# Attention scores of several heads computed side by side on TensorE, each head into a PSUM bank of its own

## The reference

```
# local attention: 6 query heads of 64 over 2 key/value heads, ALiBi, window 128, a sink per head
scores = einsum(q, k) * 64**-0.5 + bias          # head h uses key/value head h // 3
p = exp(scores - m); probs = p / (sum(p) + exp(sink - m))
out_a = probs @ v
# differential attention: 4 heads, each with two query/key maps of 32 and one value of 64
a = softmax(einsum(q, k) * 32**-0.5 - slope * dist)    # for both maps
out_c = rms_norm((a[0] - lam * a[1]) @ v) * (1 - lambda_init)
# the third mixer is a bidirectional state space model (Mamba-2): conv, decays, chunks of 128
x = x + concat(out_a, out_b, out_c) @ w_out
x = x + experts(rms_norm(x))
```

## Time and profile before

| | us |
|---|---|
| median of 3 runs | 1340.1 |
| the three runs | 1339.53, 1340.10, 1346.42 |
| profiled execution, its own time | 1351.05 |
| its span, first to last instruction | 1349.3 |
| TensorE busy (matmuls) | 1016.5 (75% of the span) |
| VectorE busy | 382.1 (28%) |
| ScalarE busy | 191.6 (14%) |
| mean granted clock of TensorE | 0.885 of full speed |
| DMA: bytes moved, mean rate | 437.50 MB, 324 GB/s |

### The profile page before, as it was taken

One profiled execution on the slowest core, in us unless ns is written; L12 is line 12 of the kernel. 1 busy time (PEld: TensorE's weight loads), 2 busy tenths in 40 slices (PEclk: granted clock), 3 DMA queues, 4 the chain that ended last, 5 costly groups with the idle time before them and its releaser, 6 DMA issues.

```text
span 1349.3 us, 26710 instructions
## 1 busy us (share of the span) xinstructions
PE 1016.5 (75%) x11124; PEld 639.6 (47%) x11124; DVE 382.1 (28%) x1160; ACT 191.6 (14%) x549; POOL 9.1 (1%) x28
## 2 busy tenths in 40 slices
PE   5999977766667887767679999766775767766864
PEld 5877753333334443334358777534432433333432
DVE  4456451211212222111144465512111111111112
ACT  2144210000000111000021443100000000000001
POOL 2000000000000000000000000000000000000000
PEclk9899989878888999977979999779877888888887
DMA  9822129999999989799993220289999999999992
GB/s 324 343 93 84 45 88 367 425 424 424 426 426 424 404 335 426 310 403 414 411 377 125 74 115 33 94 347 425 424 425 425 425 424 424 424 426 426 424 419 115
DMA packets 46015, 437.50 MB, mean 324 GB/s; under 512 B 8064, under 2 KB 10112, under 8 KB 21248
## 3 DMA queue, kind: packets, MB, share of 16 engines
q1 hardware_dynamic: 45824, 434.72, 78.1%
HBM read 433.65 MB, written 1.05 MB: 322 GB/s over the span
## 4 chain that ended last, share of the span: by engine, by line
PE 58%; DMA 22%; issue 13%; DVE 5%; ACT 1%; DVEq 1%; ACTq 0%
DMA ring<-in_w_up 22%; PE ps L465 20%; PE ps L537 7%; PE ps L476 7%; PE ps L485 4%; PE ps L446 4%; PE ps L654 4%; PE ps L549 2%; PE ps L609 2%; PE ps L583 1%; PE ps L594 1%; PE ps L553 1%; PE ps L453 1%; PE ps L616 1%; PE ps L633 1%
## 5 line engine op out<-in xcount | busy, mean ns | idle before, releaser
L465 PE MATMUL ps<-ring,xg 128*32 128x256 f32 x4096 | 337.7, 487 | 240.6 <-issue 173.3
L465 PEld LDWEIGHTS ps<-ring,xg 128*32 128x32 f32 x4096 | 173.2, 138 | 386.5 <-issue 348.7
L943 DVE SCALAR_TENSOR_TENSOR gu<-th,ps 128x128 f32<-128x128 f32 x72 | 20.7, 287 | 704.1 <-ACT th L750 704.1
L476 PE MATMUL ps<-ring,actT 128*32 128x256 f32 x2304 | 139.2, 382 | 15.2 <-issue 12.9
L750 ACT ACTIVATE th<-ps 128x128 f32<-128x128 f32 x72 | 20.0, 277 | 609.5 <-PE ps L465 609.5
L476 PEld LDWEIGHTS ps<-ring,actT 128*32 128x32 f32 x2304 | 69.0, 109 | 76.3 <-issue 20.5
L537 PE MATMUL ps<-hT,ring 128*128 128x256 f32 x416 | 97.6, 395 | 1.3 <-DVE hT L993 1.3
L537 PEld LDWEIGHTS ps<-hT,ring 128*128 128x128 f32 x416 | 81.4, 199 | 13.5 <-ACT aneg L788 2.1
L446 PE MATMUL ps<-xh,Pb 128*32 128x256 f32 x1024 | 81.1, 400 | 2.4 <-issue 2.4
L485 PE MATMUL ps<-ysb,PwT 32*128 32x256 f32 x1024 | 75.5, 404 | 2.5 <-issue 1.5
L485 PEld LDWEIGHTS ps<-ysb,PwT 32*128 32x128 f32 x1024 | 47.3, 186 | 32.5 <-issue 29.0
(11 more groups left out here) (249 smaller groups left out, 831.5 us busy)
## 6 DMA issues: line engine op xcount, KB each, us to landing
ring<-in_w_gate SPq DMA_DIRECT2D x64, 2048.0 KB, 23.7
ring<-in_w_up SPq DMA_DIRECT2D x64, 2048.0 KB, 25.1
ring<-in_w_down SPq DMA_DIRECT2D x64, 2048.0 KB, 19.3
ring<-in_w_in SPq DMA_DIRECT2D x8, 2048.0 KB, 19.2
ring<-in_w_out SPq DMA_DIRECT2D x4, 2048.0 KB, 19.7
ring<-in_w_in SPq DMA_DIRECT2D x2, 1584.0 KB, 14.6
x<-in_x SPq DMA_DIRECT2D x1, 1024.0 KB, 5.1
out<-fin SPq DMA_DIRECT2D x2, 512.0 KB, 2.7
```

The costliest lines, as they stand in the source:

```text
L465: last = mm(b_gate[j * SLOTS:(j + 1) * SLOTS, 0:2 * GQ], tokens[:, k, :], ring[:, low:high + 1:high - low, o:o + GQ], start=(k == 0), stop ...
L476: last = mm(b_y[j * SLOTS:(j + 1) * SLOTS, 0:DQ], actT[:, c * SLOTS:(c + 1) * SLOTS], ring[:, slot, o:o + DQ], start=(c == 0), stop=(c == ...
```

## The change

The scores leave the steps `sc.u` on TensorE. Five new steps compute them in groups: `aS.0` to `aS.2` two local heads each, one from each key/value head, so on array rows 0 to 63 and 64 to 127; `cS.0` and `cS.1` four units of two differential heads each, on the four groups of 32 rows. Within a group the matmuls alternate between the units, and each unit writes its own bank. VectorE and ScalarE keep their steps `sc.u`, in the old order; VectorE's now waits for the whole group.

Local unit `u` is now head `HEAD[u]` (0, 3, 1, 4, 2, 5), so that two units in a row come from both key/value heads. The two heads of an `oa` step then no longer fill one block of `mixT`, and ScalarE copies the two halves apart. Banks no longer go round: a step takes the bank whose last reader comes first in `ORDER`, and a group may hold several. `pT.6` moves ahead of the second differential group.

```diff
 ORDER = """
...
-    cv nm.5 oa.0 ybn pT.4 pT.5 sc.7 oa.1 yT.0 sc.8 nm.6 yT.1 oa.2 sc.9 sc.10 nm.7 sc.11 pT.6 outA.0 sc.12 pT.7
+    cv nm.5 oa.0 ybn pT.4 pT.5 sc.7 oa.1 yT.0 sc.8 nm.6 yT.1 oa.2 pT.6 cS.1 sc.9 sc.10 nm.7 sc.11 outA.0 sc.12 pT.7
...
+HEAD = [i % A_KV * REP + i // A_KV for i in range(A_H)]
+def tenants(step):
+    if step[0] == "aS":
+        return [("sc", A_KV * step[1] + i) for i in range(A_KV)]
+    if step[0] == "cS":
+        return [("sc", A_H + 4 * step[1] + i) for i in range(4)]
+    return [step]
+def read_at(tenant):
+    at = AT[tenant]
+    if tenant[0] == "pT" and tenant[1] >= 2:
+        h = tenant[1]
+        at = max(at, AT["oa", min(h // 2 - 1, 2)] if h < A_H + 2 else AT["od", h - A_H - 2])
+    return at
...
-        BANK[_s] = _n % 8 if _i < FIRST_OUT else 4 + _n % 4
+            _b = min(range(0 if _i < FIRST_OUT else 4, 8), key=lambda k: (read_at(_held_by[k]) if k in _held_by else -1, k))
+        BANK[_t] = _b
+        if _b in _held_by and _s[0] != "outB":
+            HELD.setdefault(_s, []).append(_held_by[_b])
+        _held_by[_b] = _t
...
+                    elif kind == "aS":
+                        if s[1] == 0:
+                            pe.wait_ge(done["act"], nth(li, "act", ("ak",)))
+                        for t in range(TT):
+                            for g in range(A_KV):
+                                r = slice(g * A_D, (g + 1) * A_D)
+                                last = mm(ps[BANK["sc", A_KV * s[1] + g]][:, t * SEQ:(t + 1) * SEQ],
+                                          aqT[r, s[1], t * P:(t + 1) * P], akT[r, :], start=True, stop=True)
+                    elif kind == "cS":
+                        pe.wait_ge(done["act"], nth(li, "act", ("ck", s[1])))
+                        for t in range(TT):
+                            for i in range(4):
+                                r = slice(i * C_QK, (i + 1) * C_QK)
+                                last = mm(ps[BANK["sc", A_H + 4 * s[1] + i]][:, t * SEQ:(t + 1) * SEQ],
+                                          cqT[r, s[1], t * P:(t + 1) * P], ckT[r, s[1], :], start=True, stop=True)
...
-                        last = A(mixT[:, s[1], :], bank[:, 0:SEQ], ACT.Copy)
+                        for h in HEAD[A_KV * s[1]:A_KV * s[1] + A_KV]:
+                            half = slice(h % 2 * A_D, (h % 2 + 1) * A_D)
+                            last = A(mixT[half, h // 2, :], bank[half, 0:SEQ], ACT.Copy)
...
+                        dve.wait_ge(done["pe"], nth(li, "pe", ("aS", u // A_KV) if u < A_H else ("cS", (u - A_H) // 4)))
```

More of the change, by code:

```diff
@@ L100 @@
 STEPS = [(name, *map(int, index)) for name, *index in (step.split(".") for step in ORDER.split())]
-ON_PE = {"xT", "xbc", "dt", "cq", "aq", "ak", "cum", "xs", "cb", "row", "sc", "y", "vz", "pT", "ck", "cv", "oa", "od",
+ON_PE = {"xT", "xbc", "dt", "cq", "aq", "ak", "cum", "xs", "cb", "row", "aS", "cS", "y", "vz", "pT", "ck", "cv", "oa", "od",
          "yT", "cT", "outA", "outB", "fT", "lg", "seed", "rank", "ov"}
@@ L155, in reader @@
     return "dve" if step[0] in ("dt", "cum", "sc", "y", "lg", "rank", "ov") else "act"
+PE_STEPS = list(COUNT["pe"])
+FIRST_OUT = PE_STEPS.index(("outA", 0))
+AT = {step: i for i, step in enumerate(STEPS)}
+HEAD = [i % A_KV * REP + i // A_KV for i in range(A_H)]
[11 more added lines that the diff above has]
+    return at
+BANK, HELD = {}, {}
+_held_by = {}
+for _i, _s in enumerate(PE_STEPS):
+    if _s[0] == "seed":
+        continue
+    for _t in tenants(_s):
+        if _s[0] in ("outA", "outB"):
+            _b = _s[1]
+        elif _s[0] == "ov":
+            _b = 7
+        else:
+            _b = min(range(0 if _i < FIRST_OUT else 4, 8), key=lambda k: (read_at(_held_by[k]) if k in _held_by else -1, k))
[3 more added lines that the diff above has]
+        _held_by[_b] = _t
 def build_encoder(nc, x_in, cols, rows, w_in, w_out, w_router, w_gate, w_up, w_down, final_w, out):
@@ L502, in _ @@
                     bank = ps[BANK[s]] if s in BANK else None
-                    if s in HELD:
-                        held = HELD[s]
+                    for held in HELD.get(s, ()):
                         pe.wait_ge(done[reader(held)], nth(li, reader(held), held))
@@ L595, in _ @@
                                           start=(n == 0), stop=(n == 2))
[L596 to L607, removed]
-                        for t in range(TT):
-                            last = mm(bank[:, t * SEQ:(t + 1) * SEQ], ql[:, t * P:(t + 1) * P], kr, start=True, stop=True)
+                    elif kind == "aS":
+                        if s[1] == 0:
+                            pe.wait_ge(done["act"], nth(li, "act", ("ak",)))
+                        for t in range(TT):
+                            for g in range(A_KV):
[9 more added lines that the diff above has]
+                                          cqT[r, s[1], t * P:(t + 1) * P], ckT[r, s[1], :], start=True, stop=True)
                     elif kind == "pT":
@@ L621, in _ @@
                         pe.wait_ge(done["act"], nth(li, "act", ("pT", 2 * c + 1)))
-                        for half in range(2):
-                            h = 2 * c + half
+                        for g in range(A_KV):
+                            half = HEAD[A_KV * c + g] % 2
                             for kc in range(TT):
-                                g = h // REP
                                 last = mm(bank[half * A_D:(half + 1) * A_D, 0:SEQ], vz[:, kc, g * A_D:(g + 1) * A_D],
-                                          ptb[h % 2][:, kc, :], start=(kc == 0), stop=(kc == TT - 1))
+                                          ptb[g][:, kc, :], start=(kc == 0), stop=(kc == TT - 1))
                     elif kind == "od":
@@ L844, in _ @@
                         if u < A_H:
-                            last = A(nmx[:, 2, u, :], nmx[:, 1, u, :], ACT.Exp, bias=rowp[:, R_SK + u:R_SK + u + 1])
+                            last = A(nmx[:, 2, u, :], nmx[:, 1, u, :], ACT.Exp, bias=rowp[:, R_SK + HEAD[u]:R_SK + HEAD[u] + 1])
                     elif kind == "pT":
@@ L1122, in _ @@
                             dve.drain()
-                            last = v.tensor_scalar(nmx[:, 1, u, :], nmx[:, 0, u, :], -A_SCALE, nsink[:, u:u + 1],
+                            last = v.tensor_scalar(nmx[:, 1, u, :], nmx[:, 0, u, :], -A_SCALE, nsink[:, HEAD[u]:HEAD[u] + 1],
                                                    ALU.mult, ALU.min)
```

8 lines of the change are left out of this document (4 added, 4 removed).

## The result

The changed kernel took 1359.6 us (median; 1356.5 to 1366.4) against 1343.15 for the kernel before: a ratio of 1.013, with a 95% interval of 1.0075 to 1.0185. It is slower, 5.6 us above the forecast and inside its range. Measured again the ratio was 1.0123 (1.0093 to 1.0154).

What follows compares the result with a forecast made beforehand. Mixers bound by TensorE, expert stages of fixed length by transfers; 0.3 (ScalarE) + 4.0 (bank waits) + 2.7 (clock) = 7.0 us per layer, 14 in all, 1365 us profiled, 1354 at the median. Range 1343 to 1363.

Steps and rivals of the forecast that it cites:

- The groups: Score matmuls on TensorE: four units in one step cost about what one costs, 1.1 us.
- Rival C: Score groups on TensorE: row groups run one after the other, 1360 us; chance 0.03.
- rival A: TensorE: the seven saved slots per layer count in full, 15 us off, 1325 us; chance 0.06.
- `cv`: TensorE up to `cv`: it starts 2.4 us earlier, after waits for the decay rows and for unit 5's bank.
- ScalarE up to `outA.0`: ScalarE's stretch from `oa.0` to `outA.0`: -2.4 + 1.1 (`oa.1`) + 0.8 (half copies) + 0.75 (copy of `pT.6`), +0.3 us.
- rival B: ScalarE behind `oa.0`: copy of `pT.4` starts at once, `cv`'s cut reaches `outA.0`; not slower, 1343 us; chance 0.17.
- rival D: Clock at its upper bound, 5 us per layer, with `oa.1` and `cS.1` at half clock; 1361 us; chance 0.20.
- The waits in `outA`: TensorE waits for banks of units 12 and 13, 4.0 us ahead of `outA.1`, 2.1 ahead of `outA.2`; price +4.0 per layer.
- The clock: Half clock behind new TensorE waits: 1.7 us behind the wait of 4.0, 1.0 for the others, 2.7 per layer.
- Sum: Both layers: 0.3 + 4.0 + 2.7 = 7.0 us each, 14 us slower in all, 1354 us.
- The expert stage: Behind the mixers: fixed length set by transfers, so it passes on the mixers' shift and gives nothing back.

Runs made afterwards that it cites:

- e0: The changed kernel as it is, measured again; 1.0123 of the kernel before.
- e1: The changed kernel with units 10 to 13 of `cS.1` in banks 1, 2, 3, 5 instead of 3, 5, 1, 2; 0.9981 of the kernel before.
- e3: The changed kernel with eight unread matmuls in the wait ahead of `outA.1` and four ahead of `outA.2`; 1.0052 of the kernel before.
- e6: e5 with the matmuls of a group unit by unit, no longer turn by turn; one run, 1341.0 us.
- e5: e2 with `cS.1` moved ahead of `pT.6`; 0.9973 of the kernel before.
- e2: e1 with other banks also for `pT.5`, `pT.6`, `oa.1`, `yT.0` and `yT.1`; 0.9969 of the kernel before.
- e7: e5 with unread matmuls in TensorE's gaps, one ahead of `oa.2` and three ahead of `cS.1`; 0.9942 of the kernel before, again 0.9939.
- e4: The changed kernel with each `oa` copied once and whole instead of in two halves, result not that of the reference; one run, 1363.7 us.
- e8: The kernel before with two unread matmuls ahead of `pT.6`; 0.9979 of the kernel before.

## Why the prediction was right

I take its steps in their order. The mechanism held at each; the clock's term was too small, and so was the smaller one ahead of `outA.0`.

**The groups.** Forecast 1.1 us, measured 1.15 in the trace's duration, where a single unit has 1.13 (1.06 to the start of the next step); a group of two has 1.13 and 1.06 as well. The Trainium skill, "TensorEngine Tiling (Array Packing)", section Theoretical Speedup, gives up to 4x for a contraction of 32 rows; four units of 1.13 in 1.15 us are 3.9x, so the trace agrees. Rival C falls with it, and rival A does too: the speed was there and the time wasn't.

**`cv`.** Forecast 2.4 us earlier; measured 2.25 in the first layer (47.87 instead of 50.12 behind `cb.0`) and 1.9 in the second. The waits that I put there are there: 0.70 of `y.2` for the decay rows, and 0.29 and 0.66 of `cv` for unit 5.

**ScalarE up to `outA.0`.** Forecast +0.3, measured +0.49 and +1.32, and +0.57 to +1.54 in e0, e1 and e3, which have the same steps up to there. The delay by `oa.1` was 1.26 (forecast 1.1), and this refutes rival B, whose test was the start of that copy. A half copy costs 0.39 more and not 0.27, so the three cost 1.17 and not 0.8. The copy of `pT.6` ahead of `outA.0` took 0.60 and ended 0.05 before it. With these sizes the sum for the first layer is -2.25 + 1.26 + 1.17 + 0.75 = +0.9; where the other 0.4 went I haven't traced. In the second layer `oa.1` took 1.57 us and `cS.1` 1.74, partly at half clock, which I had given to rival D.

**The waits in `outA`.** Forecast 4.0 and 2.1, measured 3.77 and 1.93, in both layers and in both traces of the changed kernel. At full clock (e3) `outA.2` starts 19.20 us behind `outA.0`; forecast 19.5. The price of the stretch is 42.71 - 39.14 = 3.57 us per layer against the 4.0 forecast. By e1 the waits alone are worth 42.71 - 36.65 = 6.1, of which two saved slots and what goes with them give back 2.5. The Trainium skill, same page, section Restrictions and Gotchas, warns of the pressure on PSUM. The trace agrees in part: the group does hold four banks at once, but e1 holds the same four and loses nothing. The loss lies in which unit got which.

**The clock, the term that was mis-sized.** I took 2.7 us per layer, 5.4 in all. Behind `outA.0`'s start the changed kernel loses, against e3, 45.98 - 42.71 = 3.27 in the first layer and 5.86 in the second. Before had 1.69 of its own in the first, so the change adds 7.4. What was missing is `outB`: it too ran partly at half clock, 8.86 instead of 7.17 us in both layers, 3.4 in all, which I had not counted. Without it the change adds 4.1. A second error went the other way and hid part of the first: I doubled a layer that had no fall before, though the earlier trace rows showed one in the other, so I charged 1.7 us that before was paying already. The fall also reached the router's two steps of the first layer, which took 5.0 us longer (5.89 and 6.54 us instead of 3.73 and 3.70); the wait of 3.98 ahead of the ranking was gone in return, and the first gather came 1.0 us later behind `fT`, within the 568 us.

**Sum.** To `outA.0` 1.8 (forecast 0.6), waits 7.1 (8.0), clock 7.4 (5.4): 16.4 us against 14. The rest of the 5.6 us between forecast and median is the base: the runs of before that the forecast started from had a median of 1340.1, and later medians of the same kernel were 1343.15 to 1346.65. The ratio is the better measure of the forecast: 1354/1340.1 is 1.0104, and 1.013 and 1.0123 were measured. That the profiled execution (1361.93) came near the 1365 of the forecast is luck: from trace to trace the span grew by 10.9 us only, since 5.5 of the mixers' 16.4 were made up in steps that the change doesn't touch.

**The expert stage.** It took up nothing that the traces can show between the layers (568.06 and 567.93 us, in a scatter of some us). The last one, from its first gather to the end of the last matmul, was 466.4 us long and 468.4 before. I haven't traced these 2 us; one trace of each kernel can't tell them from chance.

## What to carry to other kernels

Steps that run side by side hold several banks at once. Give these by when each reader will be done, in the order of the reader's queue: here the same step with two pairs of banks exchanged was worth 1.4% of the kernel. A slot saved on a busy engine counts only until another engine's chain is late; look for the first step whose operand comes from elsewhere, and don't multiply slots by their length. A new wait on TensorE has two prices, itself and the clock behind it. They were about equal here, and a few unread matmuls in the gap took away the second.

## What the hardware showed that I had not expected

- Two copies on ScalarE of 64 partitions cost 0.77 us, one of 128 partitions with the same 256 columns 0.38. Half the partitions save nothing.
- The order of matmuls within a group made almost no difference: 1.15 us turn by turn, 1.17 unit by unit (e6, four units of 32 rows).
- `outB` stands behind the same wait of 0.69 us in all kernels. It took 8.86 us in the changed kernel and in e5, and 7.17 in before, e1, e2, e3, e6 and e7. In e5 the first fall was 30 us ahead of it and the clock was 1.00 from 150 to 157 us, and it was slow all the same. That the clock had fallen earlier in the stretch doesn't decide it: it had in the first layer of before (`outA.0` 7.11), in e6 (5.96 and 5.79) and in the first layer of e4 (`outA.2` 8.45), and `outB` took 7.17 there. What decides it stays open.
- Before paid a fall of the clock at `outA.0` in one layer and not in the other with the same waits. With two unread matmuls ahead of `pT.6` (e8) neither layer of the one trace has it.
